# Token norm inside the down product's block, its last two slabs tile by tile, the next projection's first product chunk by chunk, and states in eight loads

## The reference, cut to what matters

```python
def post_norm(x, h, g, b):
    return layer_norm(ALPHA * x + h.astype(x.dtype), g, b)

def one_block(xb):                       # experts, 128 tokens
    ...
    h = jax.nn.gelu(jnp.einsum('td,ted->te', xb, u_tab[eidx]).astype(F32))
    w = (gates * h).astype(xb.dtype)
    return jnp.einsum('te,ted->td', w, v_tab[eidx])
...
yp = post_norm(yp, peer_ffn(yp, ...), ln_g[l, 2], ln_b[l, 2])    # this norm is moved
# next layer: proj = jnp.einsum('btd,de->bte', x, w_in)
```

## Time and profile before

| | us |
|---|---|
| median of three runs | 2296.65 (2293.35 to 2297.12) |
| profiled execution, device time | 2289.42 |
| its span, first to last instruction | 2287.7 |
| PE busy in it | 2195.6 |
| mean granted clock of TensorE | 0.984 |

### The profile page before, as it was taken

One profiled execution on the slowest core, in us unless ns is written; L12 is line 12 of the kernel. 1 busy time (PEld: TensorE's weight loads), 2 busy tenths in 40 slices (PEclk: granted clock), 3 DMA queues, 4 the chain that ended last, 5 costly groups with the idle time before them and its releaser, 6 DMA issues. The chain is left out here.

```text
span 2287.7 us, 46295 instructions
## 1 busy us (share of the span) xinstructions
PE 2195.6 (96%) x15489; PEld 1977.0 (86%) x15489; DVE 1668.7 (73%) x3921; ACT 1314.3 (57%) x3004; POOL 1012.8 (44%) x812
## 2 busy tenths in 40 slices
PE   8989899999999999999979899999999999999998
PEld 8879699999999877888879877999999997788886
DVE  5866488969999556666646555899599995566666
ACT  5545365557776555555546544645677764555554
POOL 5764347987777500000043243489877773000000
PEclk9999999999999999999989899999999999999999
DMA  7448454554444655555544593455544446555553
GB/s 266 144 148 315 180 178 141 173 174 156 152 156 156 210 194 186 183 186 190 184 137 143 181 362 112 148 166 169 171 153 154 156 148 226 189 191 183 187 189 120
DMA packets 111929, 409.33 MB, mean 179 GB/s; under 512 B 16442, under 2 KB 18658, under 8 KB 106466
## 3 DMA queue, kind: packets, MB, share of 16 engines
q1 hardware_dynamic: 107744, 391.45, 50.4%
q0 software_dynamic: 4032, 15.86, 2.1%
HBM read 397.11 MB, written 10.14 MB: 178 GB/s over the span
## 5 line engine op out<-in xcount | busy, mean ns | idle before, releaser
L2025 POOL TENSOR_TENSOR slab_ring_lo<-slab_ring,u_hi 128x512 fp32r<-128x512 f32 x512 | 677.8, 1347 | 176.1 <-ACT u_hi L2121 174.7
L2067 PE MATMUL banks<-operand_hi,u_hi 128*128 128x264 f32 x2048 | 594.2, 290 | 2.7 <-POOL slab_ring_lo L2025 2.7
L2069 PE MATMUL banks<-operand_hi,slab_ring_lo 128*128 128x264 f32 x2048 | 583.4, 285 | 0.0
L2068 PE MATMUL banks<-operand_lo,u_hi 128*128 128x264 f32 x2048 | 582.6, 284 | 0.0
L270 POOL TENSOR_TENSOR slab_ring_lo<-slab_ring,slab_hi 128x512 fp32r<-128x512 f32 x161 | 216.1, 1346 | 637.9 <-ACT slab_hi L260 637.2
L2477 DVE TENSOR_TENSOR operand_lo<-slab_ring,operand_hi 128x512 fp32r<-128x512 f32 x512 | 352.9, 692 | 129.7 <-ACT operand_hi L2442 114.9
L2525 PE MATMUL banks<-operand_hi,w_hi 128*128 128x512 f32 x1024 | 409.4, 400 | 10.2 <-DVE w_lo L2473 10.1
L2527 PE MATMUL banks<-operand_lo,w_hi 128*128 128x512 f32 x1024 | 407.1, 398 | 0.0
L2526 PE MATMUL banks<-operand_hi,w_lo 128*128 128x512 f32 x1024 | 406.9, 397 | 0.0
L2121 ACT ACTIVATE u_hi<-slab_ring 128x512 fp32r<-128x512 f32 x512 | 322.1, 631 | 121.7 <-PE banks L2069 120.9
L2067 PEld LDWEIGHTS banks<-operand_hi,u_hi 128*128 128x128 f32 x2048 | 386.8, 189 | 4.6 <-POOL slab_ring_lo L2025 3.7
(11 more groups left out here) (405 smaller groups left out, 3707.2 us busy)
## 6 DMA issues: line engine op xcount, KB each, us to landing
slab_ring<-in_u SPq DMA_DIRECT2D x256, 512.0 KB
slab_ring<-in_v SPq DMA_DIRECT2D x256, 512.0 KB
slab_ring<-in_proj SPq DMA_DIRECT2D x144, 512.0 KB
cache_k_T<-in_cache_k SPq DMA_DIRECT2D x16, 1024.0 KB, 8.7
cache_v<-in_cache_v SPq DMA_DIRECT2D x16, 1024.0 KB, 13.4
memory_T<-in_mem POOLq DMA_DIRECT2D x2, 1024.0 KB, 5.1
sample_state<-in_state POOLq DMA_DIRECT2D x1, 2048.0 KB, 12.1
out_mem_k_out<-mem_k_T SPq DMA_DIRECT2D x16, 128.0 KB, 2.2
```

Of the source, the lines that this page charges most:

```text
L2025: nc.gpsimd.tensor_tensor(step.ring_lo[:, s, g * HC:(g + 1) * HC, :], step.slab(s)[:, g * HC:(g + 1) * HC, :], hi[:, buf].bitcast(F32), AL ...
L2067: nc.tensor.matmul(bank, hi[:, buf, k, :], xh[:, c, :], start=(c == 0), stop=False)
L2068: nc.tensor.matmul(bank, hi[:, buf, k, :], xl[:, c, :], start=False, stop=False)
L2069: last = nc.tensor.matmul(bank, step.ring_lo[:, s, c, :], xh[:, c, :], start=False, stop=(c == DC - 1))
```

## The change

1. **States in eight loads.** POOL's late loads are issued behind its splits 1, 3, 5, 7 and 9 (memory, mask, inverse counts, pooling weights, context) and the state in eight parts of 256 KB behind its splits 11 to 18. The context gets a semaphore of its own, on which ACT and DVE wait in the next block.
2. **First slab of v split in the up block.** While PE runs up product 127, ACT makes the high parts of slab 0 of v and of its activations, DVE the low ones; `down` of slab 0 reads them. In the down block ACT starts with slab 1 and copies `dense` behind it. SP's store of `dense` and POOL's `fetch(0)` now wait for the first down product (`s_y`, 2).
3. **Last two slabs tile by tile.** For tile 0 slabs 126 and 127 with both halves (12 matmuls), then the same for tile 1.
4. **The norm in the down block.** The class `TokenNorm` appends its work to each engine's list in the block of `peer_down`. DVE does the residual and moments of tile 0 behind the end of that tile. DVE no longer normalizes whole tiles: it makes a reciprocal and a shift (128x1), ACT applies them to both halves of tile 0 and the second half of tile 1, DVE normalizes the first half of tile 1.
5. **Next projection's first product chunk by chunk.** PE multiplies slab 0 of the next layer with each chunk of x as soon as it is split, at the end of the down block; `window_in` starts with product 1.

```diff
-                late_loads = ((mem[:], "mem", mem_ready), (pw[:], "pool_w", late), (inv[:], "inv_count", late),
-                              (smask[:], "scan_mask", late), (s_ext[:, :, :, 0:CTX], "pool_ctx", late),
-                              (s0[:], "state", state_ready))
+                late_loads = {1: (mem[:], io["mem"], mem_ready), 3: (smask[:], io["scan_mask"], late),
+                              5: (inv[:], io["inv_count"], late), 7: (pw[:], io["pool_w"], late),
+                              9: (s_ext[:, :, :, 0:CTX], io["pool_ctx"], ctx_ready)}
+                PART = NS // STATE_PARTS
+                for k in range(STATE_PARTS):
+                    some = slice(k * PART, (k + 1) * PART)
+                    late_loads[11 + k] = (s0[:, some], io["state"][:, some], state_ready)
...
@@ window_in
-                for j in range(12):
+                for j in range(1, 12):
...
@@ peer_up, scalar
+                if n == NKEYS - 2:
+                    act.wait_ge(s_ga, GROUPS)
+                    nc.scalar.activation(wh[:], big[:, 0, 0:TP], ACT.Copy).then_inc(s_wh, 1)
+                    step.wait_slab(act, base + NKEYS)
+                    for g in range(2):
+                        nc.scalar.activation(hi[:, g], step.slab(v_slot)[:, chunks_of(g), :], ACT.Copy).then_inc(s_vh, 1)
@@ peer_up, vector
+                if n == NKEYS - 2:
+                    dve.wait_ge(s_wh, 1)
+                    nc.vector.tensor_tensor(wl[:], big[:, 0, 0:TP], wh[:].bitcast(F32), ALU.subtract)
+                    for g in range(2):
+                        dve.wait_ge(s_vh, g + 1)
+                        nc.vector.tensor_tensor(step.ring_lo[:, v_slot, chunks_of(g), :], step.slab(v_slot)[:, chunks_of(g), :],
+                                                hi[:, g].bitcast(F32), ALU.subtract).then_inc(step.v_split, 1)
@@ peer_down, sync
+            sp.wait_ge(s_y, 2)
             sp.wait_ge(s_dense, 1)
             sp.dma_start(step.hidden, dense).then_inc(s_out, 16)
...
+            norm.sync(sp)
@@ peer_down, gpsimd
-            for j in range(NB):
+            for j in range(1, NB):
                 fetch(j)
+            pool.wait_ge(s_y, 2)
+            fetch(0)
@@ peer_down, tensor
-            for s in range(SLOTS):
-                down(NKEYS // SLOTS - 1, s, False, s == SLOTS - 1)
+            for s in range(SLOTS - 2):
+                down(NKEYS // SLOTS - 1, s, False, False)
+            for t in range(2):
+                for n in (NKEYS - 2, NKEYS - 1):
+                    b = n % 2
+                    if t == 0:
+                        pe.wait_ge(s_wl, n)
+                    for g in range(2):
+                        if t == 0:
+                            pe.wait_ge(step.v_split, 2 * (vb + n) + g + 1)
...
+                        if n == NKEYS - 1:
+                            last.then_inc(norm.tile_done, 1)
+            norm.tensor(pe)
@@ TokenNorm.vector
+        residual(0)
+        moments(0)
+        residual(1)
+        scale_and_shift(0)
+        moments(1)
+        scale_and_shift(1)
+        stats, mv, std, shift = self.small(1)
+        nc.vector.tensor_scalar(z[1][:, self.halves[0]], z[1][:, self.halves[0]], mv[:, 0:1], std, ALU.subtract,
+                                ALU.mult).then_inc(self.normed_v, 1)
@@ TokenNorm.tensor
+        pe.wait_ge(self.decoded, 1)
+        decoded(low_half)
+        pe.wait_ge(self.normed_a, 1)
+        turn(0, low_half)
+        pe.wait_ge(self.sums, 4)
+        decoded(high_half)
+        pe.wait_ge(self.normed_a, 2)
+        turn(0, high_half)
+        pe.wait_ge(self.normed_v, 1)
+        turn(1, low_half)
+        pe.wait_ge(self.normed_a, 3)
+        turn(1, high_half)
...
+        for c in range(DC):
+            pe.wait_ge(self.hi_a if c % 2 else self.hi_v, c // 2 + 1)
+            nc.tensor.matmul(out, wh[:, c, :], xh[:, c, :], start=(c == 0), stop=False)
+            last = nc.tensor.matmul(out, wl[:, c, :], xh[:, c, :], start=False, stop=False)
+            pe.wait_ge(self.lo_v if c % 2 else self.lo_p, c // 2 + 1)
+            last = nc.tensor.matmul(out, wh[:, c, :], xl[:, c, :], start=False, stop=(c == DC - 1))
@@ TokenNorm.scalar
+        nc.scalar.preload_act_table(ACT.Sqrt)
+        if self.next_slab is not None:
+            split_high(step, act, self.next_slab)
+        deviation(0)
+        normed(0, range(2))
+        deviation(1)
+        normed(1, (1,))
```

More of the change, by code:

```diff
@@ L1403, in _ @@
                     if j < 8:
-                        ins = nc.scalar.activation(step.q[:, j, :], ps[:, j % 4, 0:T], ACT.Copy, scale=HD ** -0.5)
+                        bank = ps[:, j % 4 if j else TokenNorm.FIRST_BANK, 0:T]
+                        ins = nc.scalar.activation(step.q[:, j, :], bank, ACT.Copy, scale=HD ** -0.5)
                     elif j < 10:
@@ L1925, in peer @@
         out_and_peer_query(step, layer, big, qT, scratch[:, 0:2 * PH * P], keys_ready)
-        peer_up(step, layer, big, qT, scratch, keys_ready, rows, gates)
-        peer_down(step, layer, big, rows, gates)
+        peer_up(step, layer, big, qT, scratch, keys_ready, rows, gates, ahead)
+        peer_down(step, layer, big, rows, gates, ahead)
 PLAIN = 48
@@ L2343, with peer_down @@
 OWN_AT, VALUES_AT, SUM_FROM, UNROLLED = 10, (12, 18), 22, 32
[L2346 removed]
+def peer_down(step, layer, big, row_index, row_gate, ahead):
     nc, io, ps = step.nc, step.io, step.ps
@@ L2366, in peer_down @@
     TOKENS_AT = (13, 16, 19, 21, 23, 25)
+    norm = TokenNorm(step, layer, z, small, base + NKEYS if layer + 1 < LAYERS else None)
     with ExitStack() as c1, nc.Block("peer_down" + L, no_gpsimd_drain=True) as block:
@@ L2430, in _ @@
                 fetch(j)
+            norm.gpsimd(pool)
         @block.scalar
@@ L2443, in high @@
                                          ACT.Copy).then_inc(s_hi, 1)
-            nc.scalar.activation(dense.rearrange("p (n t) -> p n t", t=TS), big[:, :, TP:T], ACT.Copy).then_inc(s_dense, 1)
-            for n in range(UNROLLED):
+            for n in range(1, UNROLLED):
                 high(n // SLOTS, n % SLOTS, n < SLOTS)
+                if n == 1:
+                    nc.scalar.activation(dense.rearrange("p (n t) -> p n t", t=TS), big[:, :, TP:T],
+                                         ACT.Copy).then_inc(s_dense, 1)
                 if n == SUM_FROM:
@@ L2463, in _ @@
                     high(i, s, False)
+            norm.scalar(act)
         @block.vector
@@ L2497, in _ @@
                     link = lambda ins: step.link(dve, "vector", ins)
-                    stats, mv, std = (part[0:TS] for part in small(2))
+                    stats, mv, std, shift = (part[0:TS] for part in small(2))
                     for g in range(2):
@@ L2512, in _ @@
                     low(i, s)
+            norm.vector(dve)
         @block.tensor
@@ L2518, in down @@
                 b = s % 2
-                pe.wait_ge(s_wl, n + 1)
+                if not first:
+                    pe.wait_ge(s_wl, n)
                 for g in range(2):
```

305 lines of the change are left out of this document (174 added, 131 removed).

## The result

The changed kernel takes 2279.6 us (median of four runs, 2276.9 to 2282.8) against 2296.9 for the kernel before beside it: ratio 0.993, 95% interval 0.9914 to 0.9947, so 17.3 us faster. In a second comparison on another chip (label after_again) the ratio was 0.9911 (0.9896 to 0.9926). The profiled execution of the changed kernel is 2279.52 us with a span of 2277.4 and a mean granted clock of 0.989 (before: 2289.42, 2287.7, 0.984).

A forecast was written before the change was run, and what follows sets the result against it. TensorE, busy 2195.6 of 2287.7 us, was taken as the bound, so only its idle or low-clock time pays. 4.6 + 7.5 + 8.2 - 1.2 = 19.1, less 0.4, gives 18.7: 2296.65 to 2278.0 us, range 2271 to 2287.

The forecast's parts named there:

- Part 1 (4.6): First projection: removing the state load's stall and the cold start behind it gains 4.6 us, between 2.5 and 5.
- Rival 4: First projection: small transfers or POOL's fuller rounds still hold up a slab; 0.5 instead of 4.6, 2282.1 us; chance 0.06.
- Part 2 (7.5): Seam from up to down product, both layers: less idle time and no clock fall gain 7.5 us, between 3 and 8.3.
- rival 2: Shorter seam from up to down product: the clock still falls, 2 x 1.5 back, 2281.0 us; chance 0.10.
- 0.4 a layer for what is late next: Start of the down product: deduction for later slabs, store and gathers, 0.4 us a layer, between 0 and 3.
- rival 1: Start of the down product: DMA of slabs 4 to 7 starves PE, 2.6 a layer back, 2283.2 us; chance 0.13.
- Parts 3 and 4 (8.2): Norm behind the last down product: first chunk of x earlier, 4.1 us a layer, 8.2 in all, between 6.5 and 8.8.
- Part 5 (-1.2): Next projection's product 0 among the chunks: gains 0.3, cold start on product 1 costs 1.5; -1.2, between -1.7 and +1.
- The sum, moved alike: Whole kernel: 18.7 us taken off both the profiled execution (2289.4 to 2270.7) and the median (2296.65 to 2278.0).
- The range: Whole kernel: parts' lower bounds give 10 us less gain, upper 2 more; with 2 us scatter, 2271 to 2287.
- Rival 5: Down loop: shifted instructions make PE pause 0.85 us in each of 46 turns, 20 us slower, 2317; chance 0.05.
- Rival 3: Seam, norm and state: TensorE waits for the same last engine, a quarter of their sum, 4.7, 2292.0 us; chance 0.06.

The follow-up runs named there:

- three_one_state: Changed kernel with later gathers, decoded rows moved and slab 1 split in the norm, but the state in one load: 2268.4 us, against 2262.7 with eight loads.
- states_one_load: Changed kernel with the state in one load of 2 MB as sixth late load: 2280.7 us.
- order_back: Changed kernel with the last two down slabs in the old order, both tiles of each slab: 2285.8 us, ratio 0.996 to the kernel before.
- after: First comparison and profile of the changed kernel itself, against the kernel before: 2279.6 us, ratio 0.993.
- slab4_first: Changed kernel with SP loading slab 4 of v ahead of the store of the decoded hidden values: 2285.0 us.
- gathers_late: Changed kernel with POOL's first four gathers of v moved behind its gathers of the decoded hidden values: 2273.2 us, ratio 0.9916 to the kernel before.
- decode_late: Changed kernel with DVE's decoded-token rows and gates moved into up-block turns without a gate group: 2275.1 us, beside 2279.1 for the changed kernel.
- product0_back: Changed kernel with product 0 of layer 1's first projection back in the projection's own block: 2275.9 us, ratio 0.9922 to the kernel before.

## Why the prediction was right, and where it wasn't

The prediction, 2278.0 us, is 1.6 us under the measured 2279.6, inside its range. The seams and their releasers are as forecast. But the closeness of the sum is in part luck, since several errors in it cancel:

- **Part 1 (4.6).** Right in size: 3.3 us at the mixer's block between the first two profiles, 4.3 between the means of all, 5.0 and 5.1 in the two in which it is undone (each counted from the first product), 5.7 in time in three_one_state, and 1.6 in time in states_one_load. ACT and POOL kept up, with one exception in ten profiles (1.47 us in order_back, close to the 1.5 allowed), and PEclk is 1.00 in 39 to 42. Rival 4 is out: the states no longer hold up a slab. It drew on the rule of the Trainium skill (DMA: Bandwidth & Descriptors, Rules for kernel authors) against small transfers; here eight loads of 256 KB, spread over eight later rounds, beat the one of 2 MB by 5.7 us in three_one_state. Eight small loads issued at once, or the one large load issued later, were not tried, so the size alone isn't judged. What the prediction didn't see is what stands behind: in after the first 3.3 us shrank to 1.8 by 345, and 2.7 more were lost in the up product.
- **Part 2 (7.5).** The seam is as forecast: 1.34 us of idle time (1.36 forecast) in both layers, and PEclk 1.00 behind it; rival 2 is out. The mis-sized term is the 0.4 a layer for what is late next. It was rival 1, and real: slab 4 stalls TensorE for 1.6 and 1.8 us in after. The net is 2.9 + 2.6 = 5.4 us by the first pair of traces, 6 to 7 with part 2 undone. The cause was named in part: "slab 4 is issued no earlier than before". But its place behind the store was not what made it late (slab4_first), it was the gathers beside it (gathers_late), of which the prediction said only that they keep their places.
- **Parts 3 and 4 (8.2).** Measured 4.1 in layer 0 (54.5 to 50.4 behind T, with part 5 undone) and 4.5 in layer 1: 8.7. The first chunk of x starts at T + 4.1 (1148.81), forecast T + 4.6. A reason was missing: behind the shorter wait (1.61 us) the clock stood in after, where it fell before, and that is worth about 1 us a layer, as order_back shows (3.7 and 3.4 us for a delay of 2.58). It isn't sure, since the clock fell there in 12 of 22 cases.
- **Part 5 (-1.2).** Measured -0.6 to -0.7. The forecast PEclk of 0.50 among the chunks was wrong: it is 1.00, so product 0 ends at T + 10.0 instead of 11.2, and product 1 starts at T + 14.4 instead of 15.4, released by POOL's split and cold, as forecast.
- **The sum, moved alike.** This step has no ground in the rows, and for the profiled executions it failed. The prediction took the execution profiled before as 7.2 us under its median for no reason, and moved both by 18.7. By the traces the parts gave 16.7 of the forecast 19.1 us, and 6.3 net were given back outside the change: the profiled execution is 2279.5, not 2270.7. The medians moved by 17.3, and by 21.0 in the second comparison (2300.1 to 2279.1), so 18.7 was a fair figure for them. The two profiles are closer than the medians because the one before was lucky where the one after wasn't: 1.03 against 2.27 us ahead of layer 1's gates, 0.76 against 2.18 ahead of layer 0's, each with a cold start behind it in after. The rows of a single execution bore the parts, but not the difference of two executions. Whether the change makes the long wait of layer 0 likelier isn't shown: neither of the two profiles of the kernel before has it, and three of the eight with the change and DVE's old list do.
- **The range.** Its working has a slip: the lower bounds of the parts give 8.8 us less than the sum (2.1 + 4.5 + 1.7 + 0.5), not 10, and the upper ones 4.0 more (0.4 + 0.8 + 0.6 + 2.2), not 2. The measured time lies well inside either way.
- **Rival 5** is out: no pause in each turn of a loop is in the trace after; the down product of layer 0 takes 371.7 us against 371.9. The Trainium skill (Runtime: NRT & Kernel Launch, Instruction fetch mechanics) has a taken branch whose target isn't in the fetched pages stall its engine; no such stall shows in these turns.
- **Rival 3** is out: each of the stalls touched shrank.

What stays open: why the clock falls behind one idle stretch and stands behind another as long, and with it some 1 to 3 us of each single execution; why a copy of 64x8 is short in one execution and long in another; why states_one_load cost only 1.6 us; and TensorE's second pause in slab4_first.

## What to carry to other kernels

When work is brought forward across a seam, list all that is in flight there, not only what is queued ahead of the first load: transfers wanted some 30 us later can make the one wanted now late, and moving them back cost nothing here. An idle stretch shortened from 4.00 us, behind which the clock fell each time, to 1.34, behind which it fell in none of 22 cases, is worth more than its length. For stretches between them price both, the clock standing and fallen. And take a second profile of the kernel before: here two executions of the same program differ by 2.5 us at a single wait and the clock behind it, as much as a part of the change is worth in a layer.

## What the runs showed that was not expected

- **VectorE beside GpSimd.** In DVE's old list, while POOL splits slabs without a break, small arithmetic of 128x8 to 128x16 and casts of 64x16 take 1.0 to 1.25 us in every profile, and the copies of 64x8 either 0.15 or 1.33, which varies from one execution to the next. Moved to other turns (decode_late), most of the same operations take 0.15 to 0.18 us. Moving them was worth 3.9 us of the whole.
- **The clock behind the same idle time.** Behind 1.90 us at the change of blocks near 74 it fell in after (0.51), behind 1.96 us it stood at 1.00 in before. Behind 2.32 us ahead of the products near 165 it fell in some profiles and stood in others. Among the first down slabs it stood behind 1.83 us (slab4_first) and fell behind 1.96 and 1.99 (product0_back, decode_late). Behind the transposes' wait of 1.61 us it fell in 12 of 22 cases, behind one of 1.51 in the memory attention in 16 of 28, behind the seam of 1.34 us in none of 22. Where it fell, it was at 0.50 for 3.4 us or longer.
- **Place in the queue counted for little.** With DMA at 1.02 busy and 412 GB/s a slab issued ahead of a store was used 8.5 us behind its issue, and 7.6 where it was issued behind the store; what was in flight beside it mattered (4.4 us without the gathers).
